# Sums of squares in a grouped RMS norm: added up on GpSimd first, or summed per block on TensorE

## The reference

```python
z, xbc, dt = jnp.split(u @ w_in, ...)             # z: 512 x 2048
xbc = silu(causal_depthwise_conv(xbc, conv_w, conv_b))
xs, bm, cm = jnp.split(xbc, ...)                  # xs: 2048, bm, cm: 4 groups of 128
y = ssd_chunked(xh, dt, a, bm, cm)                # 4 chunks of 128 tokens
y = y + d_skip[:, None] * xh
y = y.reshape(b, l, D_INNER) * silu(z)
yg = y.reshape(b, l, 4, 512)                      # 4 groups of 512 features
yg = yg * rsqrt(mean(yg * yg, axis=-1) + EPS)     # one factor for each token and group
y = yg.reshape(b, l, D_INNER) * norm_w
return y @ w_out
```

## Time and profile before

| | |
|---|---|
| runs, median (lowest to highest) | 1206.93 us (1206.16 to 1207.31) |
| the profiled execution, its own time | 1206.16 us |
| its span | 1204.4 us |
| TensorE busy in the span | 1157.6 us, 96% |
| VectorE, ScalarE, GpSimd busy | 671.7, 523.0, 32.6 us |
| mean granted clock of TensorE | 0.991 |

### The profile page before, as it was taken

The page is one execution under the profiler, slowest core; times in us unless marked ns, Lnnn a source line. Parts: engine busy times, 40 slices in busy tenths (PEclk is TensorE's granted clock), DMA queues, the critical chain, the costliest instruction groups (busy, mean ns, idle before and its releaser), DMA issues.

```text
span 1204.4 us, 14740 instructions
## 1 busy us (share of the span) xinstructions
PE 1157.6 (96%) x5780; PEld 965.7 (80%) x5780; DVE 671.7 (56%) x766; ACT 523.0 (43%) x613; POOL 32.6 (3%) x87
## 2 busy tenths in 40 slices
PE   5999999999999899999999999997999999999997
PEld 5877888888788688888888888887888888888885
DVE  4568777878642746556565422476556655562114
ACT  4466666667532544434444211354534444341112
POOL 5000000000100000000000000000000000000000
PEclk9999999999999899999999999999999999999999
DMA  8242343433223303333223332502232233323221
GB/s 276 62 133 86 121 137 113 137 111 135 90 70 105 105 8 134 103 104 104 90 84 104 105 105 81 174 9 70 88 105 85 91 103 104 104 72 109 99 70 70
DMA packets 85227, 122.26 MB, mean 102 GB/s; under 512 B 4150, under 2 KB 71198, under 8 KB 85182
## 3 DMA queue, kind: packets, MB, share of 16 engines
q1 hardware_dynamic: 84592, 121.37, 30.7%
q10 hardware_dynamic: 590, 0.25, 0.1%
HBM read 119.44 MB, written 2.16 MB: 101 GB/s over the span
## 4 chain that ended last, share of the span: by engine, by line
PE 90%; DVE 5%; ACT 3%; DMA 1%; issue 1%; SPq 0%; DVEq 0%; ACTq 0%
PE bank L874 25%; PE bank L269 19%; PE bank L271 19%; PE bank L270 19%; PE bank L646 2%; DVE w_lo L266 2%; PE bank L655 1%; ACT w_hi L261 1%; DMA raw<-in_ssd_w_in 1%; DVE stage L301 1%; DVE xres L304 1%; PE bank L1035 1%; PE bank L600 1%; PE bank L333 1%; PE bank L573 1%
## 5 line engine op out<-in xcount | busy, mean ns | idle before, releaser
L269 PE MATMUL bank<-h_hi,w_hi 128*128 128x512 f32 (+1 forms) x1056 | 403.4, 382 | 12.7 <-DVE h_lo L345 9.2
L271 PE MATMUL bank<-h_hi,w_lo 128*128 128x512 f32 (+1 forms) x1056 | 399.4, 378 | 0.0
L270 PE MATMUL bank<-h_lo,w_hi 128*128 128x512 f32 (+1 forms) x1056 | 399.0, 378 | 0.0
L266 DVE TENSOR_TENSOR w_lo<-raw,w_hi 128x2048 fp32r<-128x2048 f32 x92 | 210.8, 2291 | 244.1 <-ACT w_hi L261 243.8
L380 DVE SCALAR_TENSOR_TENSOR tmp<-bank,par,tmp 128x511 f32<-128x511 f32 (+2 forms) x248 | 185.2, 748 | 129.4 <-ACT tmp L371 116.5
L261 ACT ACTIVATE w_hi<-raw 128x2048 fp32r<-128x2048 f32 x92 | 175.3, 1905 | 175.0 <-PE bank L874 158.1
L269 PEld LDWEIGHTS bank<-h_hi,w_hi 128*128 128x128 f32 x1056 | 200.6, 190 | 51.0 <-DVE w_lo L266 7.2
L271 PEld LDWEIGHTS bank<-h_hi,w_lo 128*128 128x128 f32 x1056 | 200.4, 190 | 36.8
L270 PEld LDWEIGHTS bank<-h_lo,w_hi 128*128 128x128 f32 x1056 | 200.6, 190 | 35.1
L371 ACT ACTIVATE tmp<-bank,par 128x512 f32<-128x512 f32 x112 | 86.6, 774 | 259.4 <-PE bank L271 259.3
L874 PE MATMUL bank<-w_hi,act_hi 128*128 128x512 f32 x352 | 110.7, 395 | 0.0
(11 more groups left out here) (161 smaller groups left out, 964.4 us busy)
## 6 DMA issues: line engine op xcount, KB each, us to landing
raw<-in_ffn_w_up SPq DMA_DIRECT2D x44, 1024.0 KB, 5.1
raw<-in_ffn_w_down SPq DMA_DIRECT2D x22, 1024.0 KB, 5.0
raw<-in_ssd_w_in SPq DMA_DIRECT2D x20, 1024.0 KB, 5.6
decay<-ac_dram SPq DMA_DIRECT2D x16, 512.0 KB, 3.9
raw<-in_ssd_w_out SPq DMA_DIRECT2D x8, 1024.0 KB, 5.0
from_start<-ac_dram SPq DMA_DIRECT2D x32, 128.0 KB, 3.8
xres<-in_x SPq DMA_DIRECT2D x4, 512.0 KB, 8.1
result<-xres SPq DMA_DIRECT2D x4, 512.0 KB, 2.6
```

Source lines behind the costliest of these rows:

```text
L266: dve.tensor_tensor(lo[:], raw[n % 2][:], hi[:].bitcast(F32), ALU.subtract).then_inc(lo_ready, 1)
L269: pe.matmul(dst, wh, xh, start=first, stop=False, **kw)
L270: pe.matmul(dst, wh, xl, start=False, stop=False, **kw)
L271: return pe.matmul(dst, wl, xh, start=False, stop=last, **kw)
```

## The change

The squares of every block now go to sq, and sq_sum and GpSimd's adds are gone. sums_pe is called for each of the 16 blocks, one block behind, ahead of y_pe, and for the last one in out_open_pe. Each call has 4 products and puts its 4 columns beside those of the other blocks of its group, 16 columns in all. A new step on VectorE, gsum_dve, adds the four blocks' columns with one reduce out of PSUM into group_ms; the square root reads group_ms then. sums_pe waits for the square of its block; at the first block of a new group it also waits for the reduce of the group before (gsum_ready). y_pe no longer waits for grms_ready. The buffers of the softplus steps now have places of their own, where they shared theirs with sq_sum.

```diff
--- before.py
+++ after.py
@@ -140,10 +140,8 @@
             sq = sb("sq", [P, T], scope=scope)
             group_scale = sb("group_scale", [P, T], scope=scope)
             SM = [P, NCH, HEADS]
-            with ExitStack() as softplus:
-                v_dt, e_dt, u_dt, d_dt = (sb(n, SM, scope=softplus) for n in ("v_dt", "e_dt", "u_dt", "d_dt"))
-            sq_sum = sb("sq_sum", [P, T], scope=scope)
-            l_dt, z_dt = (sb(n, SM, scope=scope) for n in ("l_dt", "z_dt"))
+            v_dt, e_dt, u_dt, d_dt, l_dt, z_dt = (sb(n, SM, scope=scope) for n in
+                                                  ("v_dt", "e_dt", "u_dt", "d_dt", "l_dt", "z_dt"))
             dt, a_dt, a_cum, to_end, chunk_decay = (sb(n, SM, scope=scope) for n in
                                                     ("dt", "a_dt", "a_cum", "to_end", "chunk_decay"))
             end_dt = sb("end_dt", [P, len(OFF), HEADS], scope=scope)
@@ -208,7 +206,7 @@
         diff_ready, relu_ready, exp_ready, m_ready = sem("diff_ready"), sem("relu_ready"), sem("exp_ready"), sem("m_ready")
         fs_ready, yo_mm, yd_mm, gate_ready = sem("fs_ready"), sem("yo_mm"), sem("yd_mm"), sem("gate_ready")
         y_step, y_done = sem("y_step"), sem("y_done")
-        ysq_ready, ysq_added, sum_mm = sem("ysq_ready"), sem("ysq_added"), sem("sum_mm")
+        ysq_ready, sum_mm, gsum_ready = sem("ysq_ready"), sem("sum_mm"), sem("gsum_ready")
         grms_ready, grr_ready, spread_mm, gs_ready = sem("grms_ready"), sem("grr_ready"), sem("spread_mm"), sem("gs_ready")
         yn_ready, y_hi_ready, y_ready = sem("yn_ready"), sem("y_hi_ready"), sem("y_ready")
 
@@ -609,24 +607,17 @@
             block_product(pe, bank[:, Z_BANK, :], n % 2, p % 2).then_inc(z_done, 1)
 
 
-        def squares_added(p):
-            return (QPG - 1) * (p // QPG) + max(p % QPG - 1, 0)
-
-        def sums_pe(pe, g):
-            p = QPG * g + QPG - 1
-            if g < G - 1:
-                pe.wait_ge(ysq_added, squares_added(p + 1))
+        def sums_pe(pe, p):
+            pe.wait_ge(ysq_ready, p + 1)
+            if p < IB - QPG:
                 pe.wait_ge(y_step, 3 * p + 1)
-                parts = [sq_sum]
-            else:
-                pe.wait_ge(ysq_added, squares_added(p))
-                pe.wait_ge(ysq_ready, p + 1)
+            if p == IB - QPG:
                 pe.wait_ge(off_ready, 3 * G)
-                parts = [sq_sum, sq]
+            elif p % QPG == 0 and p:
+                pe.wait_ge(gsum_ready, p // QPG)
             for c in range(NCH):
-                for part in parts:
-                    mm = pe.matmul(bank[:, sum_bank(g), c:c + 1], part[:, cs(c)], ones[:, 0:1],
-                                   start=part is parts[0], stop=part is parts[-1])
+                at = NCH * (p % QPG) + c
+                mm = pe.matmul(bank[:, sum_bank(p // QPG), at:at + 1], sq[:, cs(c)], ones[:, 0:1], start=True, stop=True)
             mm.then_inc(sum_mm, 1)
 
         def sum_bank(g):
@@ -638,8 +629,6 @@
                 pe.wait_ge(off_ready, 3 * (p // QPG + 1))
             if p:
                 pe.wait_ge(y_step, 3 * (p - 1) + 1)
-            if p % QPG == 1 and p > QPG:
-                pe.wait_ge(grms_ready, p // QPG)
             for c in range(1, NCH):
                 froms = [i for i, (a, b) in enumerate(OFF) if b == c]
                 for i in froms:
@@ -670,8 +659,8 @@
         def scan_pe(pe, k):
             x_tok_pe(pe, k)
             z_pe(pe, k)
-            if k % QPG == 0 and k:
-                sums_pe(pe, k // QPG - 1)
+            if k:
+                sums_pe(pe, k - 1)
             y_pe(pe, k)
             if k % QPG == 1 and k > QPG:
                 spread_pe(pe, k // QPG - 1)
@@ -708,26 +697,13 @@
 
         def square_act(act, p):
             act.wait_ge(y_done, p + 1)
-            if p % QPG == 0:
-                if p:
-                    act.wait_ge(sum_mm, p // QPG)
-                act.activation(sq_sum[:, :], xbc[:, p, :], ACT.Square).then_inc(ysq_ready, 1)
-            else:
-                if p > 1:
-                    act.wait_ge(ysq_added, squares_added(p))
-                act.activation(sq[:, :], xbc[:, p, :], ACT.Square).then_inc(ysq_ready, 1)
-
-        def add_squares_pool(pool, p):
-            pool.wait_ge(ysq_ready, p + 1)
-            if squares_added(p):
-                pool.wait_ge(ysq_added, squares_added(p))
-            pool.tensor_tensor(sq_sum[:, :], sq_sum[:, :], sq[:, :], ALU.add).then_inc(ysq_added, 1)
+            if p:
+                act.wait_ge(sum_mm, p)
+            act.activation(sq[:, :], xbc[:, p, :], ACT.Square).then_inc(ysq_ready, 1)
 
         def rms_act(act, g):
-            act.wait_ge(sum_mm, g + 1)
-            if g < G - 1:
-                act.wait_ge(y_step, 3 * QPG * (g + 1) + 1)
-            act.activation(group_ms[:, g, :], bank[:, sum_bank(g), 0:NCH], ACT.Sqrt, bias=eps[:, 0:1],
+            act.wait_ge(gsum_ready, g + 1)
+            act.activation(group_ms[:, g, :], group_ms[:, g, :], ACT.Sqrt, bias=eps[:, 0:1],
                            scale=1.0 / (D_INNER // G)).then_inc(grms_ready, 1)
 
         def group_scale_act(act, g):
@@ -821,6 +797,11 @@
             dve.wait_ge(gate_ready, p + 1)
             dve.tensor_tensor(xbc[:, p, :], tmp[:, 2, :], gate[:, :], ALU.mult).then_inc(y_done, 1)
 
+        def gsum_dve(dve, g):
+            dve.wait_ge(sum_mm, QPG * (g + 1))
+            dve.tensor_reduce(group_ms[:, g, :], bank[:, sum_bank(g), 0:QPG * NCH].rearrange("p (q c) -> p c q", c=NCH),
+                              mybir.AxisListType.X, ALU.add).then_inc(gsum_ready, 1)
+
         def grr_dve(dve, g):
             dve.wait_ge(grms_ready, g + 1)
             dve.reciprocal(group_ms[:, g, :], group_ms[:, g, :]).then_inc(grr_ready, 1)
@@ -852,6 +833,8 @@
             if k + 1 < IB:
                 mask_dve(dve, k + 1)
             y_off_dve(dve, k)
+            if q == 0 and g:
+                gsum_dve(dve, g - 1)
             if k % 2 == 1:
                 split_lo(dve, n)
             y_dve(dve, k)
@@ -914,7 +897,7 @@
         def out_open_pe(pe):
             pe.wait_ge(y_step, 3 * IB - 1)
             out_chunk(pe, 0, 3)
-            sums_pe(pe, G - 1)
+            sums_pe(pe, IB - 1)
             pe.wait_ge(gate_ready, IB)
             out_chunk(pe, 0, 2)
             spread_pe(pe, G - 1)
@@ -1172,9 +1155,6 @@
                 step(pool.affine_select(out=win_carry[:, g, :], in_=win_carry[:, g, :], compare_op=ALU.is_ge,
                                         fill=0.0, base=-(P + 1 - w), pattern=[[-1, EDGE]], channel_multiplier=1))
             pool.sem_inc(win_ready, 1)
-            for p in range(IB - 1):
-                if p % QPG:
-                    add_squares_pool(pool, p)
 
         @block.tensor
         def _(pe):
@@ -1380,6 +1360,7 @@
                 scan_dve(dve, k)
             norm_dve(dve, 10)
             norm_dve(dve, 11)
+            gsum_dve(dve, G - 1)
             grr_dve(dve, G - 1)
             for p in range(IB - QPG, IB):
                 norm_dve(dve, p)
```

## The result

Beside the kernel before, on one chip, the changed kernel took a median of 1220.22 us over 4 runs (1216.76, 1218.18, 1222.26, 1222.47) against 1206.55 (1205.84 to 1207.31). The ratio is 1.0098, with a 95% interval from 1.0074 to 1.0122: slower by about 12 us, where 9.8 were forecast. The ratio is that of the means, and takes in 26 executions of the changed kernel, the four among them; its interval reaches down to 8.9 us, so it holds the forecast too. A second set of 6 runs (e1) has a median of 1217.33 us and a ratio of 1.0099 [1.0081, 1.0117]. The changed kernel's times fall into two heaps. Of the 26 executions, 18 took 1215.7 to 1218.2 us with a mean granted clock of 0.988 to 0.991, and 8 took 1221.2 to 1223.0 with 0.985 to 0.988.

A forecast was written before the change was run, and what follows sets the result against it. TensorE was taken as the bound, busy 1157.6 of 1204.4 us. Added calls 9.79, block 15 0.86 and the last call -0.85 gave 9.80; 1206.16 + 9.80 + 0.77 for the median made 1216.7 us, range 1214.0 to 1219.3.

The forecast's parts named there:

- A call costs 0.89 us on TensorE: In the scan, each added 4-product sums_pe call costs 0.89 us, mainly weight loading; 11 count in full, 9.79 us.
- Block 15 gives no cover: The twelfth call delays y_off and so w_lo; TensorE's 2.02 us idle time moves and covers nothing, +0.86 us.
- The last call's half: Behind the scan, the last sums call has 8 records instead of 16: -0.85 us.
- The reduce: Four added VectorE reduces, 0.25 us each plus 0.1 handover, hidden under other work: counted as 0.
- the added waits: sums_pe's 15 waits for squares and the gsum_ready waits at blocks 5, 9, 13 end before they matter: 0.
- the lost adds: The 11 GpSimd adds go; nothing waited for them in time and VectorE gets nothing back: 0.
- The sum: All terms together: 9.79 + 0.86 - 0.85 = 9.80 us slower.
- with its clock granted in full: TensorE's clock in the scan and opening of the output product, as profiled before the change; no clock change was priced.
- the rivals: Not slower, 1206.1 us (5%); dearer by less, 1212.6 (5%); late squares, 1227.4 (2%); block 15 covered, 1215.8, inside the range.
- the range that I gave: Median of the changed kernel between 1214.0 and 1219.3 us, including some 0.8 us for the spread of runs.

The follow-up runs named there:

- e1: The changed kernel timed again with no edit, 6 runs against the kernel before: median 1217.33 us, ratio 1.0099.
- e2: Kernel before plus 4 unused products of a constant 128 x 128 matrix at the 12 scan blocks without sums, adds kept: 1217.33 us against 1206.94.
- e6: Kernel before plus the same 12 extra calls of 4 products, 128 weight columns, but in float32r instead of plain fp32: 1212.86 us, ratio 1.0049.
- e5: Kernel before plus 4 extra plain fp32 products at 12 scan blocks, with 64 weight columns instead of 128: 1216.83 us against 1206.17.
- e3: Changed kernel with VectorE's order turned round at block 15 alone, w_lo ahead of y_off: 1214.61 us, ratio 1.0076.
- e10: Changed kernel with each of the last call's 4 products done twice, 8 as before: 1217.46 us, ratio 1.0094.
- e8: Changed kernel with 11 GpSimd adds kept, into a tile nobody reads, and softplus buffers shared as before: 1217.23 us, ratio 1.0086.
- e11: Changed kernel with 8 needless 128 x 512 float32r products in TensorE's wait at block 15: 1215.45 us, ratio 1.0072.
- e4: Kernel before with a twelfth square added on GpSimd, so the last sums call has 4 products, not 8: 1205.18 us, ratio 0.9996.
- e7: Kernel before with the twelfth GpSimd add, first slab's chunk 2 at block 15, second slab's chunk 2 ahead of the spread: 1209.21 us, ratio 1.0028.
- e9: Kernel before with twelfth add and first slab's chunk 2 at block 15; second slab's chunk 2 unmoved, spread inside its chunk 3: 1205.79 us, ratio 0.9997.

## Why the prediction was right, and what it missed

**A call costs 0.89 us on TensorE: right.** Eleven of them put 214.22 - 204.40 = 9.82 us between the first transposes of blocks 1 and 15 in e1, and e2 shows that TensorE alone does it. That the weights' loading is the price is right in its main part: one load instead of two halves it (e6). Half the columns save less than half (e5). Of the Trainium skill's rule (TensorE: Matmul & The Clock Gate, LDWEIGHTS) the 107 ns for 128 columns agree with 0.111 us a record; by it 64 columns would be 53 ns, an estimate, and the records inside e5's call are 70 ns apart, with the edges of the call dearer on top.

**Block 15 gives no cover: right in its mechanism, a little off in size.** 0.86 was forecast, and e3 and e1 give 0.76, since w_lo starts 0.48 behind y_off's start in e1, where the forecast kept the 0.59 of the kernel before.

**The last call's half: -0.85 forecast, -0.89 measured** (e10 against e1).

**The reduce, the added waits, the lost adds: nothing, as forecast.** The reduce takes 0.17 us, with 2.0 us of cover left at the end; TensorE waits for no square; e8 has the adds at no price. The adds did not hold VectorE: its w_lo takes 2.29 us on average over the scan in the kernel before and in e1, which has no adds. The last add, beside y_lo, is the one that was held (2.21 us instead of 1.29, and 1.95 instead of 1.04 in e8).

**The sum:** 9.82 + 0.76 - 0.89 = 9.69 us by the rows, and 1215.93 - 1206.16 = 9.77 between the two profiled executions with the same mean clock. 9.80 was forecast. The 9.69 are what bears it out; that the times agree as closely is in part luck, for the spans from block 1 on differ by 10.0, and block 1 happened to start 0.2 earlier in e1.

**What it missed is TensorE's clock.** I took "with its clock granted in full" from the stretch before the change and priced no change in it. Of the rivals none came true. The mean of the 26 executions is 11.9 us over that of before, 2.2 above the sum. The second heap makes 1.7 of that, 8 of 26 executions with 5.5 us each; the first heap's mean is 0.5 above the sum. Half clock is seen to cost 1.55 us behind the wait at block 15 in the changed kernel's first profile, and 4.8 at the seam in e8. That the changed kernel's own second heap lies at that seam is inferred from e8 and from the heap's lower mean clock; no profile of it was taken. So the forecast's sum holds for executions with the clock of before, and the median of the first 4 runs, two of them of the second heap, lies outside the range that I gave, that of all 26 inside it.

Why the half clock at 800 us comes in some kernels and not in others isn't settled. Times of its kind never came in the sets of the kernel before or in e2, e5, e6, e10 and e11, and did in the changed kernel, e1, e3, e4 and e8 (e7's times spread over 7 us without clear heaps). Profiles show the place in e8 (4.8 us) and in e9 (3.2 us), and the eleven others have the clock in full there. The work at the seam and TensorE's wait of 1.5 us ahead of it are the same in all.

## What to carry to other kernels

A product with one moving column cost its weights here, and in plain fp32 twice what it cost in float32r. Where TensorE is the bound, sum on an idle engine first and multiply once; here 11 adds on GpSimd were free and 12 calls on TensorE cost 10.6 us (9.82 + 0.76). Before idle time is counted as cover, follow it back to the instruction that ends it: here the new work stood ahead of that one, so the idle time only moved. And a chunk moved to fill one wait may be the cover of the next (e7). Last, a gain or a loss of 1 to 3 us is better read from the stretch of the profile where it arises than from medians, which the granted clock moved by as much.

## What the runs showed of the hardware

Idle time of TensorE may be followed by half clock, and then costs more than itself. Behind a wait of 1.9 to 2.0 us at block 15 the clock was at half in four of nine profiles (the changed kernel, e2, e6 and e8), and in none of the four in which TensorE waited 1.1 us or less there (e3, e7, e9, e11). In e2 it reads

```profile
333.00:337.00 4.00, 4.00 (x12) 3.13 (x13) 3.66 (x6) 1.91 (x2) 0.00 (x0) 0.62 0.76 250
```

That such a wait brings the half clock about is likely but not shown: nine and four profiles are few, and five of the nine had the wait without it. Half clock follows other waits too: that of 4.7 us at 412 us in the kernel before (a granted clock of 0.50 from 412 to 416), that of 2.5 us in e7, and that of 1.5 us at the seam in two of thirteen profiles (e8 and e9). Filling the wait at block 15 with work that nobody needs cost nothing and left the clock full in the one profile taken (e11); that it makes the kernel faster is not shown.
